# Odd value pages and odd key groups of a paged-cache attention step issued by GpSimd, with four weight panels placed among the key groups

## The reference

```python
shift, scale, gate = adaln(c, ada_w, ada_b)        # silu(c) @ w + b, split in three
h = modulate(x, g, shift, scale)
past_m = cache_moba_kv[ia, page_table]             # 8 samples x 8 pages x 128 rows, keys and values
past_n = cache_nsa_kv[ia, page_table]              # k_cmp, v_cmp, k_sel, v_sel
o = attn_core(mq, nq, gates, past_m + own, past_n + own, o_win, ...)
x = x + gate * (o @ attn_w_out)
x = x + gate * (square(relu(h @ mlp_w1)) @ mlp_w2)
```

## Time and profile before

| | us |
|---|---|
| median of 3 runs (lowest to highest) | 1188.09 (1187.49 to 1190.92) |
| the profiled execution | 1189.66 |
| its span | 1187.9 |
| PE busy | 1026.6 (86%) |
| DVE, ACT, POOL busy | 421.4, 252.4, 121.5 |
| landings of MoBA pages in the chain that ended last | 7% of the span |
| landings of window blocks in that chain | 2% |

### The profile page before, as it was taken

The page is one execution under the profiler, slowest core; times in us unless marked ns, Lnnn a source line. Parts: engine busy times, 40 slices in busy tenths (PEclk is TensorE's granted clock), DMA queues, the critical chain, the costliest instruction groups (busy, mean ns, idle before and its releaser), DMA issues.

```text
span 1187.9 us, 20856 instructions
## 1 busy us (share of the span) xinstructions
PE 1026.6 (86%) x8308; PEld 748.3 (63%) x8308; DVE 421.4 (35%) x893; ACT 252.4 (21%) x546; POOL 121.5 (10%) x154
## 2 busy tenths in 40 slices
PE   4868999945878878997999999994679799999998
PEld 2556433422323545676888888884568588878886
DVE  0434049878042344533797310006931300000000
ACT  3234121102033432422213322005021211100000
POOL 2000000101103310000111111020002011111110
PEclk9779989977898875898999999997689899999999
DMA  9984549989997794303744434441014334543440
GB/s 326 340 280 130 179 156 346 354 301 376 404 341 235 251 307 140 89 19 60 259 147 136 143 135 142 142 140 39 4 47 141 108 106 144 154 159 120 162 144 36
DMA packets 106762, 215.10 MB, mean 181 GB/s; under 512 B 20464, under 2 KB 53040, under 8 KB 106585
## 3 DMA queue, kind: packets, MB, share of 16 engines
q0 software_dynamic: 38464, 147.96, 36.9%
q1 hardware_dynamic: 66314, 63.05, 16.6%
q10 hardware_dynamic: 1904, 2.94, 0.7%
HBM read 210.63 MB, written 7.48 MB: 184 GB/s over the span
## 4 chain that ended last, share of the span: by engine, by line
PE 69%; DMA 11%; DVE 11%; ACT 4%; SPq 2%; issue 2%; DVEq 0%; ACTq 0%; POOL 0%; POOLq 0%
PE psum L1194 20%; PE psum L1203 19%; DMA sb_arena<-in_cache_moba_kv 7%; PE psum L1386 5%; PE psum L624 4%; PE psum L772 2%; PE psum L1178 2%; PE psum L808 2%; DVE sb_sq L1932 2%; PE psum L683 2%; DVE sb_sq L1936 2%; DMA sb_arena<-in_state_nsa_win 2%; DMA sb_ring<-in_attn_ada_w 1%; PE psum L696 1%; DMA sb_arena<-in_cache_nsa_kv 1%
## 5 line engine op out<-in xcount | busy, mean ns | idle before, releaser
L1194 PE MATMUL psum<-sb_hT,sb_ring 128*128 128x264 f32 x1024 | 234.3, 392 | 13.3 <-ACT sb_hT L1433 6.8
L1203 PE MATMUL psum<-sb_arena,sb_ring 128*128 128x264 f32 x1024 | 229.1, 386 | 2.6 <-DVE sb_arena L2180 2.4
L1194 PEld LDWEIGHTS psum<-sb_hT,sb_ring 128*128 128x128 f32 x1024 | 197.7, 194 | 48.0 <-issue 6.8
L1203 PEld LDWEIGHTS psum<-sb_arena,sb_ring 128*128 128x128 f32 x1024 | 194.2, 190 | 36.3 <-issue 3.2
L624 PE MATMUL psum<-sb_cst,sb_arena 128*128 128x128 f32 (+4 forms) x457 | 77.4, 307 | 34.1 <-DMA sb_arena<-in_cache_nsa_kv 8.0
L624 PEld LDWEIGHTS psum<-sb_cst,sb_arena 128*128 128x128 f32 (+4 forms) x457 | 55.1, 154 | 54.0 <-issue 24.4
L2187 DVE SCALAR_TENSOR_TENSOR sb_xT<-psum,sb_mods,sb_xT 128x256 f32<-128x256 f32 (+1 forms) x16 | 7.7, 483 | 223.2 <-PE psum L1203 223.2
L808 PE MATMUL psum<-sb_ring,sb_hT 128*128 128x512 f32 (+1 forms) x192 | 79.4, 566 | 0.0
L683 PE MATMUL psum<-sb_ring,sb_cT 128*32 128x512 f32 x384 | 57.4, 708 | 11.3 <-DMA sb_ring<-in_attn_ada_w 10.1
L2180 DVE TENSOR_TENSOR sb_arena<-sb_arena x16 | 19.7, 1256 | 127.4 <-ACT sb_arena L1671 108.5
L808 PEld LDWEIGHTS psum<-sb_ring,sb_hT 128*128 128x128 f32 x192 | 35.5, 190 | 44.2 <-issue 39.8
(11 more groups left out here) (414 smaller groups left out, 1098.6 us busy)
## 6 DMA issues: line engine op xcount, KB each, us to landing
sb_ring<-in_mlp_w POOLq DMA_DIRECT2D x64, 1024.0 KB, 6.1
sb_arena<-in_cache_moba_kv SPq DMA_DIRECT2D x128, 256.0 KB, 7.4
sb_ring<-in_mlp_ada_w POOLq DMA_DIRECT2D x12, 2048.0 KB, 13.3
sb_ring<-in_attn_ada_w POOLq DMA_DIRECT2D x6, 2048.0 KB, 22.5
sb_ring<-in_ssm_ada_w POOLq DMA_DIRECT2D x6, 2048.0 KB, 16.9
sb_ring<-in_attn_w_in POOLq DMA_DIRECT2D x5, 2048.0 KB, 11.5
sb_arena<-in_cache_nsa_kv SPq DMA_DIRECT2D x64, 128.0 KB, 2.6
sb_ring<-in_s_w_glu POOLq DMA_DIRECT2D x16, 512.0 KB, 5.3
```

What stands on the lines that cost most here:

```text
L1194: last = mm(bank[m % 4][:, 0:T], panels[:, j, 256 * k + P * ch:256 * k + P * ch + P], hT[:, k, :], start=(k == 0), stop=(k == KC - 1))
L1203: last = mm(bank[2 * pair + c][:, 0:T], panels[:, j, 256 * f + P * c:256 * f + P * c + P], actT[:, 8 * j + f, :], start=(j == 0 and f == 0 ...
```

## The change

POOL now issues every odd value unit and every odd key group; SP keeps the even ones. The panels of ada2 stand between the first value rounds in POOL's queue, four before round 1 and two before round 2. The first four panels of ada3, which stood ahead of all key groups, now stand behind key groups 3, 7, 9 and 11. Page numbers are read four at a time by both engines. The selected values stay with SP, which now reads their numbers two and two for each group.

```diff
@@ -82,7 +82,7 @@
 KVS = 8
 KV_CMP, KV_MK, KV_MV, KV_SK, KV_WK, KV_SV, KV_WV, KV_END = 0, 32, 96, 160, 176, 184, 200, 208
 
-BY_POOL = tuple(KV_SK + u for u in range(16) if u % 4 > 1)
+BY_POOL = tuple(range(KV_MV + 1, KV_WK, 2))
 
 
 def kv_full_value(seq):
@@ -362,7 +362,7 @@
         mlp_full_at = [sem(f"mlp_full{i}") for i in range(SLOTS)]
         kv_full = [sem(f"kv_full{i}") for i in range(KVS)]
         kv_free = [sem(f"kv_free{i}") for i in range(KVS)]
-        selected_full = {i: sem(f"selected_full{i}") for i in range(KVS) if i % 4 > 1}
+        odd_full = {i: sem(f"odd_full{i}") for i in range(1, KVS, 2)}
 
         block = ctx.enter_context(nc.Block())
 
@@ -404,24 +404,23 @@
             moba = I["cache_moba_kv"][0].rearrange("n p a h d -> n p (a h d)")
             nsa = I["cache_nsa_kv"][0].rearrange("n p a h d -> n p (a h d)")
 
-            def moba_units(first, col, runs):
+            def moba_units(first, col, runs, units):
                 with sp.Fori(0, TS) as r:
                     found = runs(r)
-                    for j in range(KVS):
+                    for n, j in enumerate(units):
                         sp.wait_ge(kv_free[j], r + first // KVS + 1)
-                        sp.dma_start(kv[:, j, :], moba[found[j], :, col:col + 512].rearrange("n p c -> (n p) c")
+                        sp.dma_start(kv[:, j, :], moba[found[n], :, col:col + 512].rearrange("n p c -> (n p) c")
                                      ).then_inc(kv_full[j], 16)
 
-            def nsa_units(first, col, runs, units=range(KVS)):
+            def nsa_units(first, col, runs, units):
 
                 with sp.Fori(0, 2) as r:
                     for u in units:
-                        if u % 2 == 0:
-                            found = runs(r, u)
+                        found = runs(r, u)
                         sp.wait_ge(kv_free[u], r + first // KVS + 1)
                         for g in range(4):
                             sp.dma_start(kv[:, u, g * P:(g + 1) * P],
-                                         nsa[found[4 * (u % 2) + g], :, col:col + P].rearrange("n p c -> (n p) c")
+                                         nsa[found[g], :, col:col + P].rearrange("n p c -> (n p) c")
                                          ).then_inc(kv_full[u], 16)
 
             def window_units(first, which, order):
@@ -452,15 +451,15 @@
 
             def in_turn(at_page):
 
-                low, high = (pages_at(at_page + first, 4) for first in (0, 4 * PAGES))
+                low, high = (pages_at(at_page + first, 2) for first in (0, 4 * PAGES))
                 return [p for pair in zip(low, high) for p in pair]
 
-            moba_units(KV_MK, 0, lambda r: pages_at(r * 8, 8))
-            moba_units(KV_MV, 512, lambda r: in_turn(r * 4))
-
-            nsa_units(KV_SK, 256, lambda r, u: pages_at(r * 32 + u * 4, 8), (0, 1, 4, 5))
+            moba_units(KV_MK, 0, lambda r: pages_at(r * 8, 8), range(KVS))
+            moba_units(KV_MV, 512, lambda r: pages_at(r * 4, 4), range(0, KVS, 2))
+
+            nsa_units(KV_SK, 256, lambda r, u: pages_at(r * 32 + u * 4, 4), range(0, KVS, 2))
             window_units(KV_WK, 0, range(TS))
-            nsa_units(KV_SV, 384, lambda r, u: in_turn(r * 16 + 2 * u))
+            nsa_units(KV_SV, 384, lambda r, u: in_turn(r * 16 + 2 * u), range(KVS))
             window_units(KV_WV, 1, W_ORDER)
 
             sp.wait_ge(N.x_ready, 1)
@@ -536,19 +535,36 @@
                     load_ada(ADA1_SEQ[i - 1] - (i - 1), I["mlp_ada_w"][0], i - 1, i)
             load_ada(ADA1_SEQ[5] - 5, I["mlp_ada_w"][0], 5, 6)
             load_cmp(SEQ["cmp_p"])
+            moba_v = I["cache_moba_kv"][0].rearrange("n p a h d -> n p (a h d)")
+            selected = I["cache_nsa_kv"][0].rearrange("n p a h d -> n p (a h d)")
+
+            def odd_values(r):
+                found = pages_at(4 * (r + PAGES), 4, mybir.EngineType.Pool)
+                for n in range(4):
+                    j = 2 * n + 1
+                    pool.wait_ge(kv_free[j], r + KV_MV // KVS + 1)
+                    pool.dma_start(kv[:, j, :], moba_v[found[n], :, 512:1024].rearrange("n p c -> (n p) c")).then_inc(odd_full[j], 16)
+
+            def odd_keys(u):
+                found = pages_at(4 * u, 4, mybir.EngineType.Pool)
+                pool.wait_ge(kv_free[u % KVS], (KV_SK + u) // KVS + 1)
+                for g in range(4):
+                    pool.dma_start(kv[:, u % KVS, g * P:(g + 1) * P], selected[found[g], :, 256:256 + P].rearrange("n p c -> (n p) c")
+                                   ).then_inc(odd_full[u % KVS], 16)
+
+            pool.wait_ge(N.c_loaded, 64)
             pool.wait_ge(N.moba_scored, 1)
-            load_ada(SEQ["ada2"], I["ssm_ada_w"][0])
-            load_ada(SEQ["ada3"], I["mlp_ada_w"][1], 0, 4)
-            selected = I["cache_nsa_kv"][0].rearrange("n p a h d -> n p (a h d)")
-            pool.wait_ge(N.c_loaded, 64)
-            for first in (2, 6, 10, 14):
-                found = pages_at(4 * first, 8, mybir.EngineType.Pool)
-                for u in (first, first + 1):
-                    pool.wait_ge(kv_free[u % KVS], (KV_SK + u) // KVS + 1)
-                    for g in range(4):
-                        pool.dma_start(kv[:, u % KVS, g * P:(g + 1) * P],
-                                       selected[found[4 * (u % 2) + g], :, 256:256 + P].rearrange("n p c -> (n p) c")
-                                       ).then_inc(selected_full[u % KVS], 16)
+            odd_values(0)
+            load_ada(SEQ["ada2"], I["ssm_ada_w"][0], 0, 4)
+            odd_values(1)
+            load_ada(SEQ["ada2"], I["ssm_ada_w"][0], 4, 6)
+            for r in range(2, TS):
+                odd_values(r)
+            panel_behind = {3: 0, 7: 1, 9: 2, 11: 3}
+            for u in range(1, 16, 2):
+                odd_keys(u)
+                if u in panel_behind:
+                    load_ada(SEQ["ada3"], I["mlp_ada_w"][1], panel_behind[u], panel_behind[u] + 1)
             load_ada(SEQ["ada3"], I["mlp_ada_w"][1], 4, 6)
             for i in range(2):
                 load(SEQ["w_out"] + i, by_rows(I["attn_w_out"][0])[:, :, 512 * i:512 * i + 512])
@@ -898,7 +914,10 @@
                 for j in range(KVS):
                     seq, half, pg = KV_MV + KVS * r + j, j % 2, 4 * (r % 2) + j // 2
                     rows = slice(64 * half + 32 * (pg % 2), 64 * half + 32 * (pg % 2) + 32)
-                    pe.wait_ge(kv_full[seq % KVS], kv_full_value(seq))
+                    if seq in BY_POOL:
+                        pe.wait_ge(odd_full[j], 16 * (r + 1))
+                    else:
+                        pe.wait_ge(kv_full[j], kv_full_value(seq))
                     mm(bank[5][rows, 0:512], p_of(half, r // 2, pg), kv[:, seq % KVS, :],
                        start=(r == 0 and pg < 2), stop=(r == 7 and pg == 7)).then_inc(kv_free[seq % KVS], 1)
 
@@ -1009,7 +1028,7 @@
 
                 seq = KV_SK + n
                 if seq in BY_POOL:
-                    pe.wait_ge(selected_full[seq % KVS], 64 * (n // KVS + 1))
+                    pe.wait_ge(odd_full[seq % KVS], 16 * TS + 64 * (n // KVS + 1))
                 else:
                     pe.wait_ge(kv_full[seq % KVS], kv_full_value(seq))
                 if n >= 2:
```

## The result

The changed kernel took 1199.25 us (median of 4 runs, 1195.25 to 1212.24), the kernel before 1187.79 us beside it (4 runs); the ratio is 1.012, interval 1.0078 to 1.0163. The forecast was 1179.5 us in a range of 1172 to 1190. **The change makes the kernel slower, by 1.2%; I had the sign wrong.** Executions more than 1.5% above the fastest of the same kernel stay in the medians and are left out of the ratios (the longest, one of e8_four_fill, took 2325.41 us). The profiled execution of after took 1198.31 us (span 1196.6 us).

The account below looks back on a forecast made before the run. Bounds: full DMA up to 340 us, TensorE's waits for value pages, SP's issue queue, and ada3 panels amid value rounds. Terms 1.5 - 15.1 + 5 = -8.6 us gave 1188.09 - 8.6 = 1179.5 us, range 1172 to 1190.

Parts of the forecast that it names:

- A: Value rounds 0 to 2: odd pages between ada2's panels in POOL's queue cost +1.5 us, bounds -6 and +9.6.
- B: Value rounds 3 to 7: ada3 panels gone and issue shared, 6.2 us a round; -15.1 us, bounds -17.5 and -10.1.
- C: Key groups: four ada3 panels behind odd groups make group 13 late; +5 us, bounds 0 and 18.2 us late.
- Ahead of group 13 in POOL's queue now stand four panels and groups 5 to 11: Key groups: group 13, wanted at 393.3 us, lands behind these at 397.5 us, 4.2 us late.
- the window wait before 427.55 us: Behind the keys: panels 4 and 5, output weights and windows shift with TensorE, so this wait stays unchanged.
- D: Selected values: SP's reading two numbers twice per group costs nothing; even 0.3 us more each, 5 us in all, hides.
- those 17 us: Selected values: cover between SP's last issue at 488.5 us and TensorE's last products of them at 506 us.
- Slower: the panels starve the odd key groups: Rival, key groups: at 10.0 us a panel C costs 18.2 us, sum +4.6, 1192.7 us; chance 0.14.
- its threshold of 8.9 us a panel: Key groups: above 8.9 us for each ada3 panel the change is slower, below it faster.
- equal turns between queues: DMA engines alternate between queues packet by packet; equal turns give a panel half of 398 GB/s, 10.5 us, sum +6.6.
- The rounds stay as long as now: Rival, value rounds 3 to 7: two queues bring nothing, 7.45 us a round; sum -3.6, 1184.5 us; chance 0.16.
- the signs that I had named: Expected in the new profile: rounds some 6 us apart, products ending near 358 us, a POOL wait around group 13, some 5 us.

Follow-up runs that it names:

- e8_four_fill: Against e7: all four ada3 panels in the value rounds, behind odd pages of rounds 3 and 4, none among the keys; median 1191.22 us, ratio 1.0018.
- e2: Against the changed kernel: SP issues value rounds 0 to 2 itself, POOL sends the six ada2 panels at once; median 1201.02 us, ratio 1.0089.
- e1: Against the changed kernel: value rounds 3 to 7 load only 128 of 512 columns of each page; median 1200.61 us, ratio 1.0084.
- e4: Against the changed kernel: the four ada3 panels among the key groups load only an eighth of their rows; median 1200.95 us, ratio 1.0088.
- after_again: The changed kernel once more, word for word, as a control; median 1204.7 us, ratio 1.0133.
- d_four_numbers: Against the changed kernel: selected values' page numbers read as before, four twice for each pair of groups; median 1200.74 us, ratio 1.0101.
- k_keys_only: Against the changed kernel: all value pages by SP, six ada2 panels in one go, key groups as changed; median 1197.82 us, ratio 1.0076.
- k_four_numbers: Against k_keys_only: selected values' page numbers read as before the change, two readings of four for a pair; median 1192.48 us, ratio 1.0031.
- e6: Against the changed kernel: e2's edit, plus two ada3 panels behind round 3's odd pages, two behind key groups 3 and 7; median 1192.07 us, ratio 0.9999.
- e7: Against e6: selected values' page numbers read as before the change; medians 1186.87 us and, repeated, 1184.59 us, ratios 0.9973 and 0.9986.
- the two controls of before: The kernel before, word for word, taken twice more; medians 1188.11 us and, of one run, 1188.82 us.
- e1 to e4: e1, e2, e4 and one more: the changed kernel with two ada3 panels behind round 3's odd pages, two behind key groups 3 and 7; median 1200.45 us.

## Why the prediction was wrong

*A, +1.5 us forecast; +6 measured.* The landing was nearly right. Round 2's last wait ends 55.8 us after the scores (321.05 - 265.3), before 53.5 us (317.28 - 263.8), 2.3 us later where I had 1.5. The step that failed is "odd pages of round 2 land at about 318.7. Before, round 2's last page landed at 317.2": it compares one landing with another and leaves out the work behind. PE takes pages in order, and the first odd page is the second of the round. Before, two products were left when the wait ended; now 14 are, which end 4.3 us after it (325.36 - 321.05) instead of 1.0 us. That the order in POOL's queue is the cause is shown by e2; the split into landing and work behind it is read from these rows.

*B, -15.1 us forecast; -5.1 in the first pair of profiles.* This is the largest miss. The step is "TensorE's own round: 5.6 us from 351.65 to 357.24, the one round whose pages had all landed", carried over to all five rounds. That round is the second after the first step of the prompt's attention. The interval from round 3 to round 4 took 9.81 us in the very profile that I read, with page waits lying over part of the step; it is 11.06 us in after and in e1, where no page is waited for, and became the bound. With it the floor is 31.0 us (e1, some 3 us of it at the lower clock), so at most 11.0 us were to be had, whatever the pages do. Even my lower bound, -10.1, was too good: with pages the five rounds take 36.9 us. Of the gain, the panels' leaving brings some 2 us (40.2 and 40.6 us with SP alone, against 41.1 to 42.8 with the panels in between) and the second queue 2.6 us more (a mean of 37.8 us). "DMA: Bandwidth & Descriptors" of the Trainium skill, section "Rules for kernel authors", which allows issue time as the one gain of a second issuing engine, was closer than my sum: these 2.6 us are all that the split gave in the rounds.

*C, +5 us forecast, 0 to 18.2 as bounds; +9.1 in the first pair (61.25 to 70.3 us from the first turn to the last scores), +6 to +7 between the means of the profiles.* That the panels' bytes make the keys late holds: e4 and e8 show that the panels do this and not the alternation. The path was another than mine, and the size too. The step that failed is "Ahead of group 13 in POOL's queue now stand four panels and groups 5 to 11": it looks for the loss behind panels in POOL's own queue, once, near group 13. PE never waited for a group of POOL's. In after it waits at 395.17, 400.87, 406.69, 412.65 and 418.39 us, some 6 us apart, 6.3 us in all, for the even groups 6 to 14, which SP issues; no key group was waited for before. The same holds in the other profiles with panels of full size among the keys: every group waited for is an even one. SP's groups, which my sum let run beside at no cost, landed later than POOL's (13.2 and 10.1 us in the median from 383 to 400 us). From 380 to 400 us POOL's queue moved 6.19 of 7.68 MB and SP's 0.86 MB. The size: the four panels took 34.0 us from the first issue to the last landing (377.6 to 411.6 us), where I had 26.

Then come 7.5 us of waits for windows, where it was 2.8 us. The step "so the window wait before 427.55 us stays as it is" failed too: SP's windows are in flight while DMA is full (1.03 to 1.05 from 400 to 430 us), and one took 27.34 us to land, where the longest before took 20.3 us. SP itself was held up at them: a window's issue took up to 7.46 us (from 426.50 us).

*D, 0 forecast; 2 to 5 us by the pairs of times, 4 to 11 us of tail by pairs of single profiles.* The failed step is "hides in those 17 us". Two things were wrong. A group got 0.7 us longer (69.48 - 57.76 us over 16), not 0.3. And the cover was read off the selected groups alone, while eight windows stand behind them in SP's queue and need the buffers and a landing. The 17 us were also read from the one profile whose clock was late. Medians with and without the readings differ by 4.0 us (after_again and d_four_numbers, one batch); ratios by 0.45% (k_keys_only and k_four_numbers) and 0.26% (e6 and e7), and by 0.2% in the kernel before. Each of these differences is hardly larger than its uncertainty; all four point the same way, and the tails and SP's rows carry the argument.

The sum as measured, from the means of after and after_again against the two controls of before: A +6.6 (71.65 - 65.05), B -5.3 (37.1 - 42.4), keys +6.3 (66.15 - 59.9), tail +6.2 (79.7 - 73.55), together +13.8 us; the start of the projection moves by 13.8 us (262.25 - 248.5), the medians by 11.5 and 16.9 us (1199.25 - 1187.79, 1204.7 - 1187.79).

The outcome is that of the rival "Slower: the panels starve the odd key groups", at 0.14, but neither its path nor its size: the even groups and the windows were starved, at 7 to 9 us, less than its 18.2, and that was not what decided. The four panels landed 8.6, 6.9 and 6.9 us apart, under its threshold of 8.9 us a panel, and with A, B and D as forecast the change would have stayed ahead. The rule that argued for it, equal turns between queues, doesn't come out as the equal bytes that I made of it: within full stretches the DMA view gives 720 packets of POOL's queue and 587 of SP's (2.88 and 1.07 MB, before, 330 to 340 us), 1768 and 1889 (6.19 and 0.86 MB, after, 380 to 400 us), and 3288 and 5766 (12.29 and 2.80 MB, after, 400 to 440 us). In packets the first two are near equal and the third is not; in bytes POOL's queue has the most by far in all three. "The rounds stay as long as now" (1184.5 us) was nearest on B.

Of the signs that I had named, no ada3 panel went out before the last value round, and DMA is full from 380 to 390 us; but the rounds were not 6 us apart, the last products ended at 373.7 and not near 358 us, and no POOL key group was waited for. Neither sign that I had named as proof against me came: round 2's last wait ended at 321 us, before 325, and PE's waits for key groups made 6.3 us, not 14. What I had not listed, the length of the first step and the windows at the end of SP's queue, cost most.

What stays open: why the granted clock rises later in some executions of the same program than in others, why the medians of e1 to e4 all lie near 1200 us, and why SP's groups landed later than POOL's.
